# Two column groups side by side at the start of a fused decoder layer: their weights, the x pieces' banks and their order

## What is computed

```python
h = rmsnorm(x, pre_norm_g[l])
proj = jnp.einsum('bsd,dn->bsn', h, w_in[l])
...
mixed = (g[:, :, 0] * jnp.einsum('bsw,wd->bsd', y_a, w_branch[l, 0]) + ...)
out = jnp.einsum('bsd,de->bse', mixed, w_out[l])
x = x + rmsnorm(out, post_norm_g[l])
```

## Time and profile before

| what | us |
|---|---|
| median of 3 runs | 1099.57 (1099.27 to 1099.89) |
| the profiled execution | 1099.8 |
| its span in the trace | 1098.1 |
| TensorE busy in the span | 1087.8 (99%) |
| VectorE, ScalarE, GpSimd busy | 775.3, 533.8, 71.3 |
| mean transfer rate | 187 GB/s |

### The profile page before, as it was taken

How to read it: one execution, slowest core, us unless ns; L and a number is a source line. 1 busy time by engine, 2 the same in 40 slices (tenths; PEclk the granted TensorE clock), 3 DMA queues, 4 the chain that set the end, 5 groups by cost and what they waited for, 6 DMA issues and landing times.

```text
span 1098.1 us, 14822 instructions
## 1 busy us (share of the span) xinstructions
PE 1087.8 (99%) x5095; PEld 903.0 (82%) x5095; DVE 775.3 (71%) x1281; ACT 533.8 (49%) x707; POOL 71.3 (6%) x111
## 2 busy tenths in 40 slices
PE   9999999999999999999999999999999999999997
PEld 7898888888887888889887778888888888888886
DVE  5555446688878876667867777888788777777445
ACT  5664444545544554545446444454444444346442
POOL 1000000011111011221310000000000000000000
PEclk9999999999999999999999999999999999999999
DMA  8776666655566656657656556654655467665553
GB/s 277 203 219 193 193 192 195 179 178 172 174 173 185 175 153 175 190 173 218 191 167 193 170 156 207 195 175 131 207 169 168 144 229 250 229 195 186 193 194 110
DMA packets 113535, 205.29 MB, mean 187 GB/s; under 512 B 11160, under 2 KB 17872, under 8 KB 113104
## 3 DMA queue, kind: packets, MB, share of 16 engines
q1 hardware_dynamic: 113456, 204.69, 61.2%
q10 hardware_dynamic: 32, 0.01, 0.0%
HBM read 202.57 MB, written 2.10 MB: 186 GB/s over the span
## 4 chain that ended last, share of the span: by engine, by line
PE 97%; DVE 2%; ACT 0%; issue 0%; DMA 0%; DVEq 0%; ACTq 0%
PE stream L1463 30%; PE stream L1465 29%; PE stream L1464 29%; PE stream L1611 2%; PE mixer L1744 1%; PE stream L1612 1%; DVE area L899 1%; DVE wlo L908 1%; PE mixer L1760 0%; PE mixer L1577 0%; PE mixer L1711 0%; PE mixer L1562 0%; PE mixer L1498 0%; PE mixer L1710 0%; PE mixer L1560 0%
## 5 line engine op out<-in xcount | busy, mean ns | idle before, releaser
L908 DVE TENSOR_TENSOR wlo<-raw,whi 128x1024 fp32r<-128x1024 f32 (+1 forms) x376 | 457.9, 1221 | 278.9 <-ACT whi L597 275.2
L597 ACT ACTIVATE whi<-raw 128x1024 fp32r<-128x1024 f32 (+1 forms) x376 | 395.9, 1054 | 530.3 <-PE stream L1465 499.1
L1463 PE MATMUL stream<-whi,xboth 128*128 128x512 f32 (+1 forms) x1248 | 491.3, 394 | 0.1
L1465 PE MATMUL stream<-whi,xboth 128*128 128x512 f32 (+1 forms) x1248 | 484.4, 388 | 0.0
L1464 PE MATMUL stream<-wlo,xboth 128*128 128x512 f32 (+1 forms) x1248 | 483.7, 388 | 0.0
L1463 PEld LDWEIGHTS stream<-whi,xboth 128*128 128x128 f32 x1248 | 234.6, 188 | 51.1 <-issue 5.3
L1465 PEld LDWEIGHTS stream<-whi,xboth 128*128 128x128 f32 x1248 | 234.4, 188 | 48.7
L1464 PEld LDWEIGHTS stream<-wlo,xboth 128*128 128x128 f32 x1248 | 234.8, 188 | 45.6
L1463 PE MATMUL stream<-whi,yhi 128*128 128x512 f32 x192 | 76.7, 399 | 0.3 <-DVE ylo L1305 0.3
L1465 PE MATMUL stream<-whi,ylo 128*128 128x512 f32 x192 | 74.9, 390 | 0.0
L1464 PE MATMUL stream<-wlo,yhi 128*128 128x512 f32 x192 | 74.8, 390 | 0.0
(11 more groups left out here) (261 smaller groups left out, 626.8 us busy)
## 6 DMA issues: line engine op xcount, KB each, us to landing
raw<-in_w_in SPq DMA_DIRECT2D x286, 512.0 KB, 3.6
raw<-in_w_branch SPq DMA_DIRECT2D x48, 512.0 KB, 4.7
raw<-in_w_out SPq DMA_DIRECT2D x32, 512.0 KB, 3.7
raw<-in_w_in SPq DMA_DIRECT2D x12, 256.0 KB, 3.2
mixed<-in_x SPq DMA_DIRECT2D x8, 256.0 KB, 6.3
area<-in_x SPq DMA_DIRECT2D x2, 1024.0 KB, 7.1
out<-area SPq DMA_DIRECT2D x8, 256.0 KB, 2.3
raw<-in_dsa_w_uv SPq DMA_DIRECT2D x4, 256.0 KB, 2.9
```

The source lines that it names most:

```text
L597: nc.scalar.activation(whi[:, slot, :, 0:width], raw[:, slot, :, 0:width], ACT.Copy).then_inc(whi_ready, 1)
L908: nc.vector.tensor_tensor(wlo[:, slot, :, 0:width], raw[:, slot, :, 0:width], whi[:, slot, :, 0:width].bitcast(F32), ALU.subtract).then_in ...
L1463: nc.tensor.matmul(to, left_hi[:, kt, tokens], high, start=first, stop=False)
L1465: last = nc.tensor.matmul(to, left_lo[:, kt, tokens], high, start=False, stop=final)
```

## The change

The first four weight units are now unit 0 and unit 1 of both groups: the order of PA0's sixteen units is (group 0, rows 0), (group 1, rows 0), (0, 1), (1, 1), then rows 2 to 7 of group 0, then rows 2 to 7 of group 1. In this order k = 0 and 1 are the units that use x piece 0, k = 2 and 3 use x piece 1, and k = 4 to 9 use pieces 2 to 7. TensorE turns piece 1 between k = 0 and k = 1, and piece b behind unit k = b for b = 2 to 7. Units 0 and 1 go through `multiply_early`, which orders the products high by high (both token tiles), x low, weights low, each behind its own wait. ScalarE and VectorE treat unit b + 2 right behind x piece b, for b = 1 to 7 (and unit 2 ahead of it for b = 1). SyncE issues x piece k - 2 ahead of unit k. All x pieces go through mixer banks. Two and two filler transposes are gone. The group of 0 is taken after ten units instead of eight, and the squares and the root move back with it.

```diff
@@ -101,6 +101,7 @@
...
 PA0 = Part(0, 0, 1, 2 * FULL_UNITS, 2)
+FIRST = [(g, u) for u in range(2) for g in range(2)] + [(g, u) for g in range(2) for u in range(2, FULL_UNITS)]
 PS = PA0.next(1, FULL_UNITS, 1)
...
@@ -292,7 +293,7 @@
         stream = [[ctx.enter_context(nc.psum_tensor(f"stream{g}{t}", [P, GROUP], F32)) for t in range(TILES)]
...
         M = [ctx.enter_context(nc.psum_tensor(f"mixer{n}", [P, GROUP], F32)) for n in range(4)]
-        x_banks = [M[1], M[2], stream[1][0], stream[1][1], M[0], M[1], M[2], M[3]]
+        x_banks = [M[1], M[2], M[0], M[1], M[3], M[2], M[0], M[1]]
...
@@ -398,31 +399,28 @@
                 part_of_x = slice(n * X_COLS, (n + 1) * X_COLS)
...
-            def load_first(u, halves=(slice(None),)):
-                if u >= RING:
-                    sp.wait_ge(wlo_ready, u - RING + 1)
+            def load_first(k, halves=(slice(None),)):
+                g, u = FIRST[k]
+                if k >= RING:
+                    sp.wait_ge(wlo_ready, k - RING + 1)
                 for j in halves:
-                    sp.dma_start(raw[:, u % RING, j, :],
-                                 w_in_d[:, UNIT_KT * u:UNIT_KT * (u + 1), COL_A:COL_A + GROUP][:, j, :]
-                                 ).then_inc(half_landed[u] if j == 0 else raw_landed[u % RING], 16)
+                    sp.dma_start(raw[:, k % RING, j, :],
+                                 w_in_d[:, UNIT_KT * u:UNIT_KT * (u + 1),
+                                        COL_A + g * GROUP:COL_A + (g + 1) * GROUP][:, j, :]
+                                 ).then_inc(half_landed[k] if j == 0 else raw_landed[k % RING], 16)
             load_x(0)
-            load_first(0, (0,))
+            load_first(0, (0, 1))
+            load_first(1, (0, 1))
             load_x(1)
-            load_first(0, (1,))
-            load_first(1, (0, 1))
-            for u in range(2, 4):
-                load_x(u)
-                load_first(u)
-            for n in range(4, 6):
-                load_x(n)
-            for u in range(4, FULL_UNITS):
-                load_first(u)
-                if u < 6:
-                    load_x(u + 2)
+            load_first(2)
+            load_first(3)
+            for k in range(4, 2 * FULL_UNITS):
+                if k < X_LOADS + 2:
+                    load_x(k - 2)
+                load_first(k)
             sp.dma_start(rows[0:32, :], ml_conv_w[0].rearrange("j (b d) -> (j b) d", d=P)).then_inc(rows_landed, 16)
             sp.dma_start(rows[32:40, :], ml_conv_b[0].rearrange("(b d) -> b d", d=P)).then_inc(rows_landed, 16)
-            load_group(FULL_UNITS, PA0, 0, FULL_UNITS, w_in_d, COL_A + GROUP)
             for to, of in ((lam_in[:, :, :].rearrange("p a b -> p (a b)"), da_lambda[0].rearrange("a b -> (a b)")),
...
@@ -622,17 +620,15 @@
                 act.wait_ge(x_turned, j + 1)
...
                 round_half(0, j)
+            for j in range(2):
+                round_half(1, j)
             for b in range(1, 8):
-                if b >= 4:
-                    round_unit(PA0, 0, b - AHEAD)
                 act.wait_ge(x_turned, b + 2)
...
                 if b == 1:
-                    for j in range(2):
-                        round_half(1, j)
-                elif b < 4:
-                    round_unit(PA0, 0, b - AHEAD)
+                    round_unit(PA0, 0, 2 - AHEAD)
+                round_unit(PA0, 0, b + 2 - AHEAD)
...
@@ -645,15 +641,15 @@
                            [area0[:, t, bass.ds(i * 2 * GROUP + (of_turn * 2 + g) * GROUP, GROUP)]
...
-            for u in range(FULL_UNITS - AHEAD, FULL_UNITS):
+            for u in range(10 - AHEAD, 10):
                 round_unit(PA0, 0, u)
-                if u in (5, 6):
-                    square_x(u - 5)
+                if u in (6, 7):
+                    square_x(u - 6)
             act.wait_ge(msx_ready, 1)
...
             act.wait_ge(rstdx_ready, 2)
-            take_da(PA0, 0, 0, 0)
-            for u in range(FULL_UNITS, 2 * FULL_UNITS):
+            take_group(PA0, 0, 10, 0, [area0[:, t, 0:GROUP] for t in range(TILES)])
+            for u in range(10, 2 * FULL_UNITS):
                 round_unit(PA0, 0, u)
...
@@ -937,19 +933,17 @@
             for j in range(2):
...
                 split_half(0, j)
+            for j in range(2):
+                split_half(1, j)
             for b in range(1, 8):
-                if b >= 4:
-                    split_unit(PA0, 0, b - AHEAD)
                 dve.wait_ge(xhi_ready, 2 * b + 2)
...
                 if b == 1:
-                    for j in range(2):
-                        split_half(1, j)
-                elif b < 4:
-                    split_unit(PA0, 0, b - AHEAD)
-
-            for u in range(FULL_UNITS - AHEAD, FULL_UNITS):
+                    split_unit(PA0, 0, 2 - AHEAD)
+                split_unit(PA0, 0, b + 2 - AHEAD)
+
+            for u in range(10 - AHEAD, 9):
                 split_unit(PA0, 0, u)
...
@@ -957,7 +951,7 @@
             nc.vector.reciprocal(rstdx, rstdx).then_inc(rstdx_ready, 1)
...
             nc.vector.tensor_scalar(half_rstdx, rstdx, 0.5, None, ALU.mult).then_inc(rstdx_ready, 1)
-            for u in range(FULL_UNITS, 2 * FULL_UNITS):
+            for u in range(9, 2 * FULL_UNITS):
                 split_unit(PA0, 0, u)
...
@@ -1447,13 +1441,8 @@
             def multiply(part, i, k, u, units, bank_pair, left_hi, left_lo, width=GROUP, tiles=range(TILES)):
...
                 slot = (part.unit0 + k) % RING
-                halves = part is PA0 and k < 2
-                if not halves:
-                    pe.wait_ge(wlo_ready, part.unit(i, k) + 1)
+                pe.wait_ge(wlo_ready, part.unit(i, k) + 1)
                 for j in range(UNIT_KT):
-                    if halves:
-                        pe.wait_ge(xlo_ready, UNIT_KT * k + j + 1)
-                        pe.wait_ge(wlo_ready if j else half_wlo, k + 1)
                     kt = UNIT_KT * u + j
...
@@ -1468,6 +1457,23 @@
                 elif final:
...
+            def multiply_early(k, j):
+
+                high, low = whi[:, k, j, :], wlo[:, k, j, :]
+                pe.wait_ge(xhi_ready, j + 1)
+                pe.wait_ge(whi_ready if j else half_whi, k + 1)
+                for t in range(TILES):
+                    nc.tensor.matmul(stream[k][t][:, :], xhi[:, j, t * P:(t + 1) * P], high, start=j == 0, stop=False)
+                pe.wait_ge(xlo_ready, j + 1)
+                for t in range(TILES):
+                    nc.tensor.matmul(stream[k][t][:, :], xlo[:, j, t * P:(t + 1) * P], high, start=False, stop=False)
+                pe.wait_ge(wlo_ready if j else half_wlo, k + 1)
+                for t in range(TILES):
+                    last = nc.tensor.matmul(stream[k][t][:, :], xhi[:, j, t * P:(t + 1) * P], low,
+                                            start=False, stop=False)
+                if j == UNIT_KT - 1:
+                    last.then_inc(units_done, 1)
+
             def open_banks(part, i, k):
...
@@ -1484,15 +1490,15 @@
             keep_busy(4)
...
             nc.tensor.transpose(M[0][:, 0:KT], rows_g[:, :], ident[0:KT, 0:KT]).then_inc(cols_turned, 1)
-            keep_busy(5)
-
-            def turn_x(b):
-                pe.wait_ge(x_landed[b], 16)
-                if b == 4:
+            keep_busy(3)
+
+            def turn_x(b, halves=range(UNIT_KT)):
+                if b == 2:
                     pe.wait_ge(cols_ready, 1)
-                if b >= 5:
-                    pe.wait_ge(xlo_ready, 2 * (b - 5) + 2)
-                for j in range(2):
+                if b >= 3:
+                    pe.wait_ge(xlo_ready, b - 2 if b < 5 else 2 * (b - 4) + 2)
+                for j in halves:
+                    pe.wait_ge(x_landed[b], 16)
                     for t in range(TILES):
...
@@ -1501,16 +1507,19 @@
                         last.then_inc(x_turned, 1)
...
             turn_x(0)
-            keep_busy(6)
+            keep_busy(4)
+            multiply_early(0, 0)
+            multiply_early(0, 1)
             turn_x(1)
-            for u in range(FULL_UNITS):
-                pe.wait_ge(xlo_ready, UNIT_KT * u + (1 if u == 0 else 2))
-                multiply(PA0, 0, u, u, FULL_UNITS, 0, xhi, xlo)
-                if u + 2 < FULL_UNITS:
-                    turn_x(u + 2)
-            open_banks(PA0, 0, 1)
-            for u in range(FULL_UNITS):
-                multiply(PA0, 0, FULL_UNITS + u, u, FULL_UNITS, 1, xhi, xlo)
+            multiply_early(1, 0)
+            multiply_early(1, 1)
+            for k in range(2, 2 * FULL_UNITS):
+                g, u = FIRST[k]
+                if k <= X_LOADS + 1:
+                    pe.wait_ge(xlo_ready, UNIT_KT * u + 2)
+                multiply(PA0, 0, k, u, FULL_UNITS, g, xhi, xlo)
+                if k < X_LOADS:
+                    turn_x(k)
             open_banks(PS, 0, 0)
...
```

## The result

The changed kernel takes 1101.62 us (median of 14 runs, 1101.18 to 1102.74), the kernel before 1099.45 in the same comparison (14 runs, 1098.70 to 1100.39). The ratio is 1.0021, 95% interval 1.0014 to 1.0029: slower by 2.17 us, where +1.3 had been forecast.

What follows compares the result with a forecast made beforehand. TensorE was taken as the bound. Earlier start and stalls put the first 344-column matmul at 56.92 instead of 55.63, +1.29 us on 1099.80: 1101.09, as a median 1100.9; own range 1100.3 to 1101.5, 8 in 10 1098.8 to 1102.0.

Steps and rivals of the forecast that it cites:

- Bound: Whole kernel: TensorE, busy 1087.8 of 1098.1 us, sets the end; opening gains or losses at the first 344-column matmul stay.
- Term 1, the earlier start: Opening: four fillers fewer and x piece 1 turned after unit 0; first product at about 6.5 instead of 8.13 us.
- Term 2, the clock: Opening: TensorE's clock still rises at 9.85 us, so unit 0 ends 0.89 earlier; net gain about 0.4 us.
- T(0): Time at which the last matmul of unit 0 has been streamed on TensorE; 11.73 us before, forecast 10.84.
- the rival by which it follows the first product: Opening: the clock rises 1.72 us after the first product, at 8.2; all behind comes 0.74 earlier, 1100.1 us; chance 0.18.
- Terms 3, 4 and 6: Load order, mixer banks for x pieces, and squares, root and eviction moved back two units: each claimed to cost nothing.
- Term 5, the chain of 3.83: ScalarE and VectorE: weights rounded behind x piece b start unit b + 2 no earlier than 3.83 us after unit b; stalls 1.90.
- the rival without stalls: Opening: weights ready in time, the chain does not bite; sixteen units end at 54.99, giving 1098.9 us; chance 0.12.
- late-clock rival: Opening: a wait at the first product delays the clock's rise to 12.4 us; 1.0 more, 1101.9 us; chance 0.06.

Runs made afterwards that it cites:

- e1: Changed kernel with weight unit b + 2 rounded and split ahead of x piece b (unit 3 still behind piece 1); median 1099.15 us, 0.57 under the kernel before.
- e5: The changed kernel as it is, run again beside the kernel before on the same chip; median 1102.51 us, 3.13 above the kernel before.
- e7: e1 with one filler transpose instead of three ahead of x piece 0; median 0.54 us above the kernel before.
- e8: Changed kernel with only unit 2 rounded and split ahead of x piece 1; median 1100.59 us, 1.21 above the kernel before.
- e4: Kernel before with all weight units rounded and split behind their x piece (units 4 to 7 were ahead); median 1.63 us above the kernel before.
- e10: Changed kernel with the eight products at about 394 us widened from 4 to 128 partitions, the rest zeros; 1100.89 us.
- e9: Kernel before with the eight products at about 394 us widened from 4 to 128 partitions, the rest zeros; 1099.21 us.
- e3: Changed kernel with the 5 and 6 filler transposes of the kernel before; median 1100.33 us, 0.61 above the kernel before.

## Why the forecast was right, and where it was short

- *Bound* (one engine, so that the opening is read at the first 344-column matmul): held. +1.56 there, +1.44 in the execution.
- *Term 1, the earlier start*: x piece 0 turned at 4.72 as worked out. The first two products start 0.99 apart (6.60, 7.59), so their effective start is 7.59 - 0.85 = 6.74 and not 6.5. Of these 0.24 us, 0.10 is the later start (6.60); 0.14 is the longer first step, which I had counted in before (8.13 for a start at 7.99) and left out here.
- *Term 2, the clock*: rise at about 10.1 instead of 9.85. T(0) = 11.04 against 10.84: 0.20 short in all. The fixed time that I took is refuted (7 to 10.1 in these traces), and so is the rival by which it follows the first product; its size was a matter of the execution, and that the rise came within 0.3 us of my 9.85 was luck. The quarter of a microsecond that I gave it was too small. I had also blamed the length of the page's slices for the clock row that reads 9 throughout; it reads 1.00 in stretches of 1 us too, so that row cannot show the opening's lower level at all.
- *Terms 3, 4 and 6*: loads, banks and square root cost nothing in after. For the loads this was closer than I said: in the kernels with the new order unit 2's weights landed between 9.8 (e1) and 11.5 (e5), 10.8 in after, and not at 10.3, so the cover is down to nothing once the chain is gone (e7, e8).
- *Term 5, the chain of 3.83*: right in place, number and size. From T(0) to the end of the opening 46.15 against 46.08 worked out, and 44.11 without the chain against 44.15 (54.99 - 10.84, from the rival without stalls). e1 takes it out of the changed kernel, e4 puts it into the old one.
- *The rest*, the step that failed: "whatever the opening gains or loses stays to the end, since no later wait is there to absorb it". No later wait changed, but a spell at the lower clock 390 us in came in 17 of 22 runs of the changed kernel and in about a quarter of the old one's. It costs 1.6 us where it comes. An estimate from the shares: 1.6 x (9/14 - 25/96) = 0.6 and 1.6 x (8/8 - 5/30) = 1.3 on top of the 1.7 us of e10 against e9 give 2.3 and 3.0, and the two comparisons measured 2.2 and 3.1. I had read the waits of TensorE and not its clock, and a single trace without the spell could not show it. My late-clock rival had the right size and the wrong place.
- Why the changed kernel meets the spell so often is shown only in part. In the ten traces it goes with the time between the first rise and the eight products, and the stalls lie between the two: they add about 2 us to that time in the changed kernel and 1 us in e4 (9 of 11). But e3 and e8 have stalls too and only 4 of 11 and 2 of 10 such runs, and when the clock rose in the runs without a trace is not on record. It was not tried to move these products alone.

So the time lies in the stated range, just beyond the forecast's own (1101.62 against 1101.5), and 2.17 us is at the very edge of what I had called no change (2.2 us): 0.92 for that was too much, and the slower side deserved the chance of a second, separate event of the clock.

## What to carry to other kernels

Where an in-order engine prepares two inputs of which one comes early (weights, prefetched) and one late (handed on by the engine that is the bound), put the early one first: behind the late one it makes a chain from the bound engine back to itself, here 3.83 us against the 3.56 that TensorE had to do in between, and a fraction of a microsecond for each unit. Such stalls do not show as idle time while records overlap; compare starts with the step of the chain. And before a difference of a few tenths of a per cent is given to an edit, count in how many runs the clock fell: here one row of a profile (the granted clock by stretches) explains up to 1.3 of a difference of 3.1 us.

## What had not been expected of the hardware

- TensorE was busy without a gap and its clock fell all the same: behind eight products with 4 rows of 128, to the lower level for seven matmuls of 512 columns and parts of two more (from about 397.9 to 401.3 in e3), in a quarter of the runs of the kernel before. With zeros in the other 124 rows, same count and columns, it fell in none of 44 runs. The Trainium skill (TensorE: Matmul & The Clock Gate, Part 1) ties such a fall to idle stretches; here none is in the trace.
- The first rise of the clock came anywhere between about 7 and 10.1 us after the start, by about a microsecond apart for one and the same kernel (after and e5). That is wider than the half microsecond that the Trainium skill gives (TensorE: Matmul & The Clock Gate, Part 1).
- The same 512 KB transfer (unit 2's weights), issued at 3.7 to 3.9 us behind the same transfers, landed after 5.9 us in one execution (e1) and, on another chip, after 6.4, 7.2 and 7.8 in three others (e7, e8, e5).
